# Output projection of the mixer layers summed part by part in PSUM, with the retention and head-sum work re-ordered around it

## The reference, cut to what matters

```python
for l in range(2):
    p = h @ w_in[l]                          # 32 column tiles in all
    ya = hgrn2(p)                            # gated linear attention, rms norm per head, * silu(gate)
    yb = gla(p)                              # the same form, other decays
    yc = rwkv7(p)                            # delta rule scan, group norm, gate
    yd = retnet(p)                           # below
    mix = concat([ya, yb, yc, yd]) @ w_out[l]        # (256,1024) @ (1024,1024)
    h = layer_norm(ALPHA * h + mix)
    h = layer_norm(ALPHA * h + (dense_ffn(h) if l == 0 else moe(h)))

def retnet(p):                               # 4 heads of 64
    q, k, v, g = split(p)
    q, k = rotary(q), rotary(k) / 8
    o = group_norm(causal(q @ k.T * decay) @ v)
    return silu(g) * o
```

## Time and profile before

| | us |
|---|---|
| Median of 3 runs | 3305.31 (3303.12 to 3308.59) |
| The profiled execution, its own time | 3310.59 |
| The span shown by its profile | 3308.9 |
| PE busy / DVE busy / ACT busy / POOL busy | 3021.8 / 1124.0 / 484.7 / 534.1 |
| Mixer layer 0: first matmul of the projection to `laA` | 1977.9 to 2264.5 |
| Output projection of layer 0 / of layer 1 starts | 2233.1 / 2791.8 |

### The profile page before, as it was taken

How to read it: one execution, slowest core, us unless ns; L and a number is a source line. 1 busy time by engine, 2 the same in 40 slices (tenths; PEclk the granted TensorE clock), 3 DMA queues, 4 the chain that set the end, 5 groups by cost and what they waited for, 6 DMA issues and landing times.

```text
span 3308.9 us, 39415 instructions
## 1 busy us (share of the span) xinstructions
PE 3021.8 (91%) x16166; PEld 1616.6 (49%) x16166; DVE 1124.0 (34%) x1889; ACT 484.7 (15%) x847; POOL 534.1 (16%) x644
## 2 busy tenths in 40 slices
PE   5998787998899999999999979978999997799996
PEld 2446554866333333333333347757887875433333
DVE  3664552012333333333333324451011553222112
ACT  1111111001101010101010112321001231211111
POOL 0000550000123223232323210101110020000000
PEclk9997778998899999999999979989999997799998
DMA  6334002435399999999999952022443211399991
GB/s 221 131 124 156 1 1 102 139 109 188 114 396 394 396 394 397 394 397 394 397 394 397 368 192 102 26 77 87 152 142 111 77 52 42 129 389 387 383 386 66
DMA packets 334383, 728.06 MB, mean 220 GB/s; under 512 B 17920, under 2 KB 63420, under 8 KB 333932
## 3 DMA queue, kind: packets, MB, share of 16 engines
q1 hardware_dynamic: 321456, 697.22, 57.0%
q0 software_dynamic: 8896, 24.59, 2.1%
q10 hardware_dynamic: 3836, 3.58, 0.3%
HBM read 708.55 MB, written 16.78 MB: 219 GB/s over the span
## 4 chain that ended last, share of the span: by engine, by line
PE 66%; DVE 3%; ACT 2%; DMA 1%; issue 1%; SPq 0%; POOL 0%; POOLq 0%; DVEq 0%; ACTq 0%; PEldq 0%
PE P L704 64%; DVE R L1572 2%; PE P L707 2%; DMA WS<-in_w_gate_up 1%; ACT R L2282 1%; ACT L2282 1%; SPq L625 0%; DVE R L1578 0%; DMA R<-expert_rows,small 0%; ACT xT L2282 0%; DMA expert_rows<-R 0%; ACT ea L2282 0%; POOL R L2801 0%; DVE R L2273 0%; DVE xT L1578 0%
## 5 line engine op out<-in xcount | busy, mean ns | idle before, releaser
L704 PE MATMUL P<-R 128*32 128x512 f32 (+10 forms) x6484 | 1281.3, 497 | 108.3 <-POOL R L2643 30.7
L704 PE MATMUL P<-WS,R 128*64 128x512 f32 (+4 forms) x4456 | 1007.4, 589 | 9.6 <-POOLq L2712 2.7
L704 PEld LDWEIGHTS P<-R 128*32 128x32 f32 (+4 forms) x6484 | 534.3, 147 | 576.7 <-issue 477.4
L704 PEld LDWEIGHTS P<-WS,R 128*64 128x64 f32 (+2 forms) x4456 | 314.3, 129 | 634.2 <-issue 619.8
L704 PE MATMUL P<-R,WS 128*128 128x256 f32 (+1 forms) x1888 | 508.5, 429 | 22.9 <-DVE R L1572 13.7
L2282 ACT ACTIVATE R<-P 128x512 f32<-128x512 f32 (+5 forms) x430 | 223.3, 521 | 2013.4 <-PE P L704 1702.8
L1572 DVE TENSOR_TENSOR R<-P,R 64x512 f32<-64x512 f32 (+4 forms) x268 | 173.1, 646 | 804.9 <-ACT R L2282 478.7
L704 PEld LDWEIGHTS P<-R,WS 128*128 128x128 f32 x1888 | 360.9, 193 | 159.9 <-issue 97.8
L704 PE MATMUL P<-xT,WS 128*128 128x256 f32 (+2 forms) x1728 | 403.3, 386 | 9.6 <-ACT xT L2282 3.5
L704 PEld LDWEIGHTS P<-xT,WS 128*128 128x128 f32 (+2 forms) x1728 | 319.0, 189 | 72.0 <-issue 21.8
L1572 DVE TENSOR_TENSOR R<-R 128x512 f32<-128x512 f32 (+9 forms) x366 | 257.7, 704 | 64.4 <-ACT R L2282 52.2
(11 more groups left out here) (164 smaller groups left out, 1015.4 us busy)
## 6 DMA issues: line engine op xcount, KB each, us to landing
WS<-in_w_gate_up SPq DMA_DIRECT2D x192, 1024.0 KB, 11.5
R<-in_w_down SPq DMA_DIRECT2D x128, 1024.0 KB, 12.9
R<-in_w_gate_up SPq DMA_DIRECT2D x64, 1024.0 KB, 14.4
WS<-in_w_in SPq DMA_DIRECT2D x60, 1024.0 KB, 7.4
WS<-in_w_mod SPq DMA_DIRECT2D x24, 1024.0 KB, 7.3
R<-in_moe_w_down SPq DMA_DIRECT2D x23, 1024.0 KB, 8.6
WS<-in_moe_w_gate SPq DMA_DIRECT2D x20, 1024.0 KB, 10.5
WS<-in_moe_w_down SPq DMA_DIRECT2D x17, 1024.0 KB, 8.1
```

The lines of the kernel that those rows point to most:

```text
L704: return nc.tensor.matmul(out, lhsT, rhs, start=start, stop=stop, skip_group_check=True)
```

## The change

1. `FILLS`: `go` is gone. `gnB` has 11 steps and `g1` to `g8` have 8 each, so the total is the same.
2. `sd` is emptied right after `weigh(1)`, ahead of the use of `rooted`; `weigh(2)` comes ahead of that use too, and ACT's `decays(2)` ahead of its logarithm of `gnB`.
3. The rotation (`rot`, now `PAIRED`) is done in span 8, between its scores and `g8`; DVE combines it there.
4. ACT empties `rv` and takes the sigmoid of retention's gate early, into a region `rg` of its own. POOL makes the three gate products with `PT` (`gate_ready`), and DVE multiplies by the inverse root `hr4` last (`gla_ready`).
5. `hn` goes to `P[6]` and `P[7]` outside the numbered jobs. `rs` is 4 jobs of two heads, `ro` is one job of four heads.
6. The output projection is summed in `P[4]` to `P[7]` (two output tiles in each bank), input tile by input tile, as soon as a part of `mixT` is there. Only the parts of tiles 6 and 7 come after `mix_ready`. DVE empties 4 banks in place of 8 halves, and both weight slots are freed at the end.

```diff
-         + [(f"{x}{c}", k) for c in range(4) for x, k in (("w", 2), ("u", 2), ("s", 3))] + [("gnA", 4), ("gnB", 7)]
-         + [(f"g{i}", 7) for i in range(1, 9)] + [("go", 12)])
+         + [(f"{x}{c}", k) for c in range(4) for x, k in (("w", 2), ("u", 2), ("s", 3))] + [("gnA", 4), ("gnB", 11)]
+         + [(f"g{i}", 8) for i in range(1, 9)])
@@ PE
+                    if i == 8:
+                        pe.wait_ge(S("p_free"), 32 * l + 28)
+                        for t in range(2):
+                            total(f"rot{l}", t, k2("rot"), [flat(PT[:, 24 + 2 * t:26 + 2 * t, :])])
                     project(l, f"g{i}")
...
-                project(l, "go")
                 pe.wait_ge(S("p_free"), 32 * (l + 1))
-                pe.wait_ge(S("vector_step"), mixed("hsq", l))
-                for i in range(2):
-                    total(f"hn{l}", i, k1("head"), [flat(g1t)[:, 512 * i:512 * i + 512]])
...
+                wo = [unit(), unit()]
+                def out_part(ks, ms):
+                    for k in ks:
+                        for m in ms:
+                            last = mm(acc(m), wproj(wo[m // 4], 512, k, 128 * (m % 4), 128 * (m % 4) + 128), mixT[:, k, :],
+                                      k == 4 and m % 2 == 0, k == 7)
+                    return last
+                out_part((4, 5), range(0, 4))
+                pe.wait_ge(S("vector_step"), mixed("hsq", l))
+                for i in range(2):
+                    mm(P[6 + i][:, :], k1("head"), flat(g1t)[:, 512 * i:512 * i + 512]).then_inc(S("hn_done"), 1)
                 pe.wait_ge(S("vector_step"), mixed("qk_ready", l))
+                for i in range(4):
+                    q, z = i // 2, i % 2
+                    hp, w = slice(64 * z, 64 * z + 64), 256 - 128 * q
+                    b = job(f"rs{l}", i)
+                    for t in range(2):
+                        last = mm(b[:, w * t:w * t + w], qk[hp, 2 + t, 128 * q:128 * q + 128], qk[hp, t, 128 * q:256])
+                    done(last)
+                pe.wait_ge(S("hn_free"), 2 * (l + 1))
+                out_part((4, 5), range(4, 8))
...
+                pe.wait_ge(S("vector_step"), mixed("gla_ready", l))
+                out_part((0,), range(8))
                 total(f"rnA{l}", 0, k1("head"), [flat(ro)])
+                out_part((1,), range(8))
                 pe.wait_ge(S("vector_step"), mixed("rc_sq", l))
                 total(f"rnB{l}", 0, k1("head"), [flat(rq)])
+                out_part((2, 3), range(8))
                 pe.wait_ge(S("vector_step"), mixed("mix_ready", l))
-                eight(f"out{l}", lambda k: mixT[:, k, :])
+                for i in range(4):
+                    done(out_part((6, 7), range(2 * i, 2 * i + 2)))
+                for i in range(2):
+                    unit_used()
@@ VectorE, after weigh(1)
+                n, b = ready(f"sd{l}", 0)
+                F(n, stt(flat(g2t[:, 0:2, :]), b[:, :], 64.0, flat(PT[:, 4:6, :])))
+                for t in range(2):
+                    n, b = ready(f"sd{l}", 1 + t)
+                    F(n, tt(g2t[:, 2 + t, :], b[:, 0:N], PT[:, 10 + t, :]))
+                weigh(2)
                 rooted()
@@ ScalarE, after the last project
+                act_.wait_ge(S("gl_score"), 8 * l + 7)
+                A(fn(rg, PT[:, 30:32, :], ACT.Sigmoid))
...
+                n, b = ready(f"rv{l}")
+                F(n, fn(vtk, b[:, :].rearrange("p (c n) -> p c n", c=2), ACT.Copy))
                 for i in range(2):
-                    log_of(f"hn{l}", i, flat(hr4)[:, 512 * i:512 * i + 512], 2 * N, 1.0, 0)
+                    act_.wait_ge(S("hn_done"), 2 * l + i + 1)
+                    mark(fn(flat(hr4)[:, 512 * i:512 * i + 512], P[6 + i][:, :], ACT.Ln, scale=1.0, bias=eps(0)), "hn_free")
                 inverse_root(flat(hr4))
@@ POOL
+                pool.wait_ge(S("scalar_step"), scalar("hg_sig", l))
+                Gm(tt(hg[:, 0:2, :], hg[:, 0:2, :], PT[:, 6:8, :]))
+                Gm(tt(hg[:, 2:4, :], hg[:, 2:4, :], PT[:, 13:15, :]))
+                mark(tt(rg, rg, PT[:, 30:32, :]), "gate_ready")
```

More of the change, by code:

```diff
@@ L420, in build @@
             jobs += [(f"lr{l}", 3), (f"kkn{l}", 1), (f"vmA{l}", l), (f"vmB{l}", l), (f"tk{l}", 3), (f"lm{l}", 8), (f"rkv{l}", 1),
-                     (f"gate{l}", 1), (f"vt{l}", 2), (f"gnA{l}", 1), (f"gnB{l}", 1), (f"sd{l}", 3), (f"hn{l}", 2),
-                     (f"rot{l}", 2), (f"rv{l}", 1), (f"rs{l}", 8), (f"ro{l}", 4), (f"rnA{l}", 1), (f"rnB{l}", 1),
-                     (f"out{l}", 8), (f"laA{l}", 1), (f"laB{l}", 1)]
+                     (f"gate{l}", 1), (f"vt{l}", 2), (f"gnA{l}", 1), (f"gnB{l}", 1), (f"sd{l}", 3),
+                     (f"rot{l}", 2), (f"rv{l}", 1), (f"rs{l}", 4), (f"ro{l}", 1), (f"rnA{l}", 1), (f"rnB{l}", 1),
+                     (f"out{l}", 4), (f"laA{l}", 1), (f"laB{l}", 1)]
             if l:
@@ L433, in build @@
         PAIRED = {f"{x}{l}" for l in range(2)
-                  for x in ("lr", "kkn", "vmA", "vmB", "tk", "lm", "rkv", "gate", "vt", "gnA", "gnB", "sd")}
+                  for x in ("lr", "kkn", "vmA", "vmB", "tk", "lm", "rkv", "gate", "vt", "gnA", "gnB", "sd", "rot")}
         def psum(stage, n):
@@ L2205, in _ @@
                 V(tt(mixT[:, 4:6, :], mixT[:, 4:6, :], oT))
-                n, b = ready(f"sd{l}", 0)
-                F(n, stt(flat(g2t[:, 0:2, :]), b[:, :], 64.0, flat(PT[:, 4:6, :])))
-                for t in range(2):
-                    n, b = ready(f"sd{l}", 1 + t)
-                    F(n, tt(g2t[:, 2 + t, :], b[:, 0:N], PT[:, 10 + t, :]))
                 dve.wait_ge(S("gl_zero"), l + 1)
-                for i in range(2, 10):
-                    if i < 9:
-                        weigh(i)
+                gather_scores(1)
+                for i in range(3, 9):
+                    weigh(i)
                     gather_scores(i - 1)
+                dve.wait_ge(S("scalar_step"), scalar("sin_ready", l))
+                V(tt(cosT, cosT, cosT))
+                V(ts(cosT, cosT, -2.0, 1.0))
+                dve.wait_ge(S("p_free"), 32 * l + 28)
+                V(tt(qk, PT[:, 24:28, :], over(4, cosT)))
+                gather_scores(8)
+                for i in range(2):
+                    n, b = ready(f"rot{l}", i)
+                    F(n, tt(rsw[:, 2 * i:2 * i + 2, :], b[:, :].rearrange("p (t n) -> p t n", t=2), over(2, sinT)))
+                mark(tt(qk, qk, rsw, ALU.add), "vector_step")
                 dve.wait_ge(S("gl_mixed"), l + 1)
@@ L2250, in _ @@
                 V(tt(rc, rc, ang[:, 0:2, :]))
-                dve.wait_ge(S("scalar_step"), scalar("rg_sig", l))
-                V(tt(rsw[:, 0:2, :], rsw[:, 0:2, :], PT[:, 30:32, :]))
-                mark(tt(mixT[:, 6:8, :], rc, rsw[:, 0:2, :]), "vector_step")
-                for m in range(8):
-                    n, b = ready(f"out{l}", m)
-                    F(n, stt(xT[:, m, :], xT[:, m, :], ALPHA, b[:, 0:N], ALU.mult, ALU.add))
+                mark(tt(mixT[:, 6:8, :], rc, rg), "vector_step")
+                for i in range(4):
+                    n, b = ready(f"out{l}", i)
+                    F(n, stt(flat(xT[:, 2 * i:2 * i + 2, :]), flat(xT[:, 2 * i:2 * i + 2, :]), ALPHA, P[4 + i][:, :],
+                             ALU.mult, ALU.add))
                 layer_norm(f"laA{l}", lambda k: ("ln1_g_2", 8 * l + k))
@@ L2603, in _ @@
                 decays(1)
+                decays(2)
                 project(l, tiles("gnB"))
@@ L2607, in _ @@
                 inverse_root(flat(gr))
-                decays(2)
                 for i in range(3, 9):
```

74 lines of the change are left out of this document (28 added, 46 removed).

## The result

The changed kernel takes 3231.45 us (median of 4 runs, 3226.99 to 3232.91), the kernel before on the same chip 3305.8. The ratio is 0.9773, with a 95% interval of 0.9756 to 0.979: 2.3% faster. Forecast were 3237 us and a range of 3230 to 3253.

A forecast was written before the change was run, and what follows sets the result against it. TensorE, busy 91% of the span, was taken as the bound, with gains only where it waits or runs slowly. Layer sums of 96.2 and 96.7 us gained 68.6 together, giving 3236.7 against the median, forecast 3237; range 3230 to 3253.

The forecast's parts named there:

- item 9: `rs` and `ro` in the tail at full clock: 4.0 us taken, bounds 3.5 to 5.3.
- items 3 to 5: `sd`, first to second span, second span to value product: 2.85, 7.16 (layer 1: 7.70) and 38.71 us.
- item 4: First span to second span with one more projection step: 7.16 us in layer 0, 7.70 in layer 1.
- The one of half a microsecond: Cover at `hn_free`: banks 6 and 7 free at 7.7 us after the value product, `rs` done at 8.0 to 8.5.
- Rival A: VectorE or ScalarE sets the time at tail joins, 3 to 10 us per layer: 3243 to 3257 us; chance 0.23.
- Item 10: The join before `laA`: 0.30 us, now once instead of twice.
- rival B: The clock does not fall at `sd`: 3.7 us more gain than forecast, 3233 us; chance 0.15.
- Rival C: Half clock in the tail, 37 us of TensorE work per layer taking 74: 3310 us; chance 0.03.
- Rival D: No effect: late weight-slot release or the experts' weight stream waits the saving away; both slots uncovered 3266 us; chance 0.04.
- (1): From `sd` on, TensorE busy in one piece for over 85 us per layer, clock 1.00 in the tail.
- (2): Third sum of `sd` 1.8 us after the first.
- (3): `laA` starts 96 us after `gnB` starts.

The follow-up runs named there:

- rot_tail: Changed kernel with the rotation back behind the value product and the transpose `rv` moved behind `hn`: 3235.41 us, ratio 0.98.
- fill_la: `fill_after_sum` with the sums of `laA` issued ahead of the two `unit_used` joins: 3226.31 us, ratio 0.9751 against the kernel before.
- after_again: The changed kernel, unchanged, measured again: 3234.28 us, ratio 0.9782 against the kernel before.
- bank_order: Changed kernel with each projection part ordered by output tile first, input tile second: 3236.61 us (3235.34 without one long execution), ratio 0.9791.
- fill_after_sum: Changed kernel with 7 of the 11 steps of `gnB` moved behind the second head sum: 3225.53 us, ratio 0.9759 against the kernel before.
- all_three: `fill_la` with the root's products on VectorE spread over spans 5 to 7: 3221.49 us, ratio 0.974 against the kernel before.
- go_back: Changed kernel with the old filler portions (`gnB` 7 steps, `g1` to `g8` 7 each, `go` 12 behind the value product): 3232.7 us, ratio 0.9786.

## Why the prediction was right

The direction, the size and the mechanism hold, with one join uncovered and one term of the sum read wrongly. By items, in the changed kernel's profile, layer 0:

| Item | forecast us | measured us |
|---|---|---|
| 1, 2: `gnB`; head sum and wait | 4.78; 3.23 | 4.74; 3.24 |
| 3: `sd` | 2.85 | 3.26 (layer 1: 2.80) |
| 4: first to second span | 7.16 | 7.37 (layer 1, forecast 7.70: 6.66) |
| 5: second span to value product | 38.71 | 38.85 |
| 6: value product, transposes | 3.54 | 3.50 |
| 7; 8: projection; `hn`, `rnA`, `rnB` | 28.1; 3.5 | 28.10; 3.53 |
| 9: `rs` and `ro` | 4.0 | 1.69 + 1.51 = 3.20 |
| waits in the tail (`hn_free`) | 0 | 0.36 |
| 10: join ahead of `laA` | 0.30 | 0.54 (layer 1: 0.45) |
| Sum, layer 0 / layer 1 | 96.2 / 96.7 | 96.69 / 95.42 |

The sum is nearer than its terms. In layer 0 item 9 was 0.8 too long, and items 3 to 5, the join and the wait were 1.4 too short, so that they nearly cancel; in layer 1, where the clock was down for a shorter time, item 4 was 1.0 too long as well.

*Covers.* A cover is the time by which another engine's chain is ready before TensorE asks for it. The one of half a microsecond did not hold and costs 0.36. ScalarE was as fast as forecast (1.28 + 2 x 0.70), and the banks were free 7.7 us after the value product, as forecast. But `rs` ends at 7.4, not at 8.0 to 8.5: the term of item 9 that is too large is the same that hid the wait at `hn_free`. `mix_ready` came with 1.3 us to spare (VectorE done at 2214.65, asked for at about 2215.98), forecast 1.5. `gla_ready` was never waited for, though POOL's gates were ready only at +5.5, just behind the forecast's 4.1 to 5.4, and VectorE waited 2.57 us for them: its product ended at 2198.72 and was asked for at 2200.23, 1.5 to spare. Rival A thus happened at one join and at a tenth of its price, and `rot_tail` shows how near it is: 3 us more per layer with the rotation put back.

*Item 9.* I called half of the old 4.21 + 2.85 a floor, 3.5. It is none: 3.20 was measured. The old rows are spans of several jobs with waits for banks inside, and half of a span with waits is no price of the work. In `rs` an instruction takes 1.69 / 16 = 0.11.

*Item 10.* The wait is 0.15 to 0.24 longer than the 0.30 of the old kernel. The profile names TensorE itself as what ends it, and `unit_used` waits until the last of the numbered matmuls is reported done. `fill_la` has VectorE's emptying unchanged and `laA` ahead of `unit_used`, and there the wait is gone. So it is this join and not VectorE; why it is longer than before is not shown.

*Items 3, 4 and rival B.* The forecast took the half clock after the wait of 2.2 us, B said that it would stay up. Both happen. Windows of TensorE alone, changed kernel in layer 0 and then `after_again` in layer 1, each behind the same wait of 2.21:

```profile
2138.00:2142.00 4.00, 4.00 (x15) 0.50 0.64 208
2142.00:2145.00 3.00, 3.00 (x15) 0.95 1.05 399
...
2185.00:2223.00 38.00, 37.57 (x213) 1.00 0.21 66
```

```profile
2658.00:2662.00 4.00, 2.32 (x9) 1.00 0.00 0
2662.00:2666.00 4.00, 3.19 (x18) 1.00 0.00 0
```

B priced only the first scores (1.85 per layer). With the clock up, the sums and the first projection steps are shorter too, and the third span's scores wait 0.73 for VectorE, so that B is worth 1.8 to 1.9 per layer (96.59 and 96.69 against 94.82), near the forecast.

*Rival C.* 1.00 from 2145 to 2223, and no instruction at the half clock in the tail. The rule of the Trainium skill (TensorE: Matmul & The Clock Gate, "psum-queue depth-cycling") that the prediction weighed there is not borne out: the parts go round four banks with the clock at 1.00, and `bank_order`, which does so less often, changes nothing.

*Rival D.* The experts start at the same distance from `laA`, and from `laA` of layer 0 to `gnB` of layer 1, with the dense network between, it is 427.46 us against 427.38. The 14.4 us of later release are hidden.

*The 5.5 us between 3237 and 3231.45.* The stretches gave 69.4 where 68.6 were forecast. The rest, some 5 us, lies outside them, where the kernels have the same instructions: the executions differ by up to 7 us before the mixer layers begin (1970.7 to 1977.9 over four profiles of the two kernels), with the time spent at the lower clock, and behind the last `laA` two profiles of the changed kernel took 484.9 and 482.8. The second measurement of the changed kernel gave 3234.28. That the sum by the median came within 0.2% is in part luck.

*The signs announced.* (1) TensorE is at work from 2134.77 to 2222.95, 88 us, with one wait of 0.36: right but for that wait (layer 1 has 0.28 more, ahead of the third sum of `sd`), and the clock was 1.00 in the tail. (2) Third sum of `sd`: 1.8 us forecast; in layer 1 the row of six large instructions starts at 2658.91 and the four small ones at 2660.87, 1.96. (3) 96.69 and 95.42 for 96. (4) The last 16 matmuls follow without a wait. (5) The windows of the tails are full, 49.4 of 50 us.

## What to carry to other kernels

When a busy engine waits for others at the end of a stage, look for its own work whose input is already complete (here a sum over parts that become ready one by one) and put it into the waits in pieces; then check each join by adding up the other engines' chain against the filler placed ahead of it, because the last tenths are lost at the thinnest cover. Put filler where the waiting engine would be idle, not where it fits in the program: the same seven steps were worth 2 to 4 us more behind the head sum than ahead of it. And before a difference in total time is credited to an edit, compare the same stretch of both traces: 8 of the 77.6 us here lay in work that no edit touched, most of it where executions of the same work differ by up to 9 us.

## What the runs showed of the hardware

**The clock after the same wait.** Behind the one wait of 2.21 us ahead of `sd` the granted clock fell to 0.50 in some layers and executions and stayed at 1.00 in others, with the same program (layer 1 of the changed kernel and of `after_again`: 3.37 and 2.03 us for the same 12 instructions). Over the seven runs in which this wait is the only long one there, it fell behind it in 8 of 14 layers. With the wait filled it did not fall in any of the six layers of `fill_after_sum`, `fill_la` and `all_three`. The Trainium skill (TensorE: Matmul & The Clock Gate, "HAM oscillation") ties the half clock to pauses of TensorE, longer ones than this; the traces agree that a pause can bring it back and that filled layers keep 1.00, and the layers that kept 1.00 behind the same pause show that here it is no certain price.

**GpSimd beside VectorE.** In the changed kernel POOL's three gate products run while VectorE squares; in `go_back` VectorE is idle through them. POOL's groups by form in layer 0, changed kernel and then `go_back`, and the three of the changed kernel by shortest, median and longest (ns):

```profile
L2668 POOL TENSOR_TENSOR R<-R 128x512 f32<-128x512 f32 x3 | 4.7, 1552 | 22.8 <-ACT R L2304 22.7
```

```profile
L2669 POOL TENSOR_TENSOR R<-R 128x512 f32<-128x512 f32 x3 | 3.8, 1265 | 27.6 <-ACT R L2305 27.4
```

```profile
L2668 POOL TENSOR_TENSOR R<-R x3: 1265/1266/2124, 2188.0 to 2191.5; 128x512 f32<-128x512 f32 x3
```

1552 ns is a mean that hides what happened: two of the three products took 1.27 us, as in `go_back`, and the second took 2.12. That one ran from 2189.3 to 2191.4, and VectorE's square of 1024 columns from 2188.88 to 2190.34; the square, which began beside the first product, took 1.46 us, and 1.23 where POOL is idle. VectorE's two additions, each with one input in PSUM, took 1.42 together in both kernels. Layer 1 has the same (1.27 twice and 2.12). By the mean the products lie just above the forecast's bounds of 1.1 to 1.54. The Trainium skill (SBUF — State Buffer, "SBUF: two separate sides") says that a VectorE instruction with two inputs in SBUF and a GpSimd instruction that reads SBUF lock each other out. The trace agrees: only the square, whose inputs both lie in SBUF, and the product beside it got longer, by 0.2 and 0.9 us.
